# Turning raw rows by a scaled diagonal, and loading gate and up weights in row halves, in a two-layer decoder trunk

## The reference, cut to what matters

```python
def rms_norm(x, gain):
    xf = x.astype(jnp.float32)
    y = xf * lax.rsqrt(jnp.mean(xf * xf, axis=-1, keepdims=True) + NORM_EPS)
    return (y * gain.astype(jnp.float32)).astype(x.dtype)
...
    for i in range(DEPTH):
        h = rms_norm(x, attn_norm[i])
        x = x + mixer_i(h, ...)          # begins with u = h @ w_in
        h = rms_norm(x, ffn_norm[i])
        x = x + hier_moe(h, ...)
...
def expert_block(args):                  # inside hier_moe, 32 experts of width 512, top 2 per token
    xblk, e = args
    hid = jax.nn.silu(xblk @ w_gate[e]) * (xblk @ w_up[e])
    return hid @ w_down[e]
```

## Time and profile before

| | us |
|---|---|
| median of 3 runs | 1724.29 |
| lowest and highest | 1724.13, 1724.97 |
| profiled execution, its own time | 1721.84 |
| its span in the trace | 1720.0 |

### The profile page before, as it was taken

One profiled execution on the slowest core, in us unless ns is written; L12 is line 12 of the kernel. 1 busy time (PEld: TensorE's weight loads), 2 busy tenths in 40 slices (PEclk: granted clock), 3 DMA queues, 4 the chain that ended last, 5 costly groups with the idle time before them and its releaser, 6 DMA issues.

```text
span 1720.0 us, 20542 instructions
## 1 busy us (share of the span) xinstructions
PE 1584.3 (92%) x7884; PEld 749.1 (44%) x7886; DVE 440.6 (26%) x1111; ACT 393.5 (23%) x879; POOL 200.6 (12%) x287
## 2 busy tenths in 40 slices
PE   6999899799999999997499989999699999999993
PEld 3545574433333333332246457855333333333331
DVE  1485651620000000000412235643500000000002
ACT  2345450311111111111100236632211111111110
POOL 2241220000000000000101012320000000000000
PEclk9999999899999999999599999999899999999997
DMA  7120307289999999999804220043599999999995
GB/s 244 50 98 7 111 4 293 98 334 420 422 421 421 421 422 422 422 422 393 225 5 152 80 65 1 2 176 141 221 398 422 421 422 422 422 422 422 422 421 199
DMA packets 110919, 468.24 MB, mean 272 GB/s; under 512 B 34105, under 2 KB 40505, under 8 KB 61708
## 3 DMA queue, kind: packets, MB, share of 16 engines
q1 hardware_dynamic: 103564, 450.67, 65.5%
q0 software_dynamic: 5120, 8.41, 1.3%
q10 hardware_dynamic: 2176, 8.39, 1.3%
HBM read 456.91 MB, written 18.91 MB: 277 GB/s over the span
## 4 chain that ended last, share of the span: by engine, by line
PE 80%; DMA 10%; DVE 4%; SPq 2%; ACT 1%; issue 1%; POOL 1%; ACTq 0%; DVEq 0%; POOLq 0%
PE bank L1734 22%; PE bank L1747 10%; PE bank L1714 9%; PE bank L1380 8%; DMA arena<-in_moe_w_up 8%; PE bank L535 6%; PE bank L774 6%; PE bank L429 4%; PE bank L394 3%; PE bank L1724 2%; PE bank L411 2%; SPq L1686 2%; PE bank L855 2%; PE bank L1740 1%; DMA arena<-y_d 1%
## 5 line engine op out<-in xcount | busy, mean ns | idle before, releaser
L1734 PE MATMUL bank<-arena 128*64 128x512 f32 x2048 | 452.6, 594 | 17.0 <-DMA arena<-in_moe_w_up 15.5
L1734 PEld LDWEIGHTS bank<-arena 128*64 128x64 f32 x2048 | 147.6, 137 | 312.6 <-issue 303.1
L1747 PE MATMUL bank<-arena 128*64 128x512 f32 x1024 | 230.6, 592 | 2.1 <-DVE arena L1836 2.1
L1832 DVE TENSOR_TENSOR arena<-arena,bank 128x256 f32<-128x256 f32 x64 | 26.9, 421 | 656.3 <-ACT arena L1822 656.3
L1753 POOL DMA_INDIRECT y_d<-arena,slot_row x64 | 62.7, 980 | 927.8 <-ACT arena L1827 927.8
L1714 PE MATMUL bank<-arena 128*64 128x512 bf16 x1152 | 153.5, 394 | 8.2 <-DVE arena L1707 8.2
L1380 PE MATMUL bank<-arena 128*128 128x512 f32 x320 | 140.6, 601 | 0.8 <-issue 0.8
L1747 PEld LDWEIGHTS bank<-arena 128*64 128x64 f32 x1024 | 71.6, 137 | 124.4 <-issue 110.8
L1822 ACT ACTIVATE arena<-bank 128x256 f32<-128x256 f32 x64 | 24.6, 384 | 420.5 <-PE bank L1734 420.5
L535 PE MATMUL bank<-arena 128*128 128x512 f32 x256 | 111.4, 593 | 0.0
L774 PE MATMUL bank<-arena 128*128 128x512 f32 (+1 forms) x288 | 105.3, 525 | 0.0
(11 more groups left out here) (282 smaller groups left out, 1440.5 us busy)
## 6 DMA issues: line engine op xcount, KB each, us to landing
arena<-in_moe_w_gate SPq DMA_DIRECT2D x64, 2048.0 KB, 21.7
arena<-in_moe_w_up SPq DMA_DIRECT2D x64, 2048.0 KB, 26.2
arena<-in_moe_w_down SPq DMA_DIRECT2D x64, 2048.0 KB, 24.4
arena<-in_even_w_in SPq DMA_DIRECT2D x4, 2048.0 KB, 8.3
arena<-y_d ACTq DMA_DIRECT2D x8, 1024.0 KB, 8.6
arena<-bias_row_d SPq DMA_DIRECT2D x2, 3584.0 KB, 11.8
arena<-in_odd_w_in SPq DMA_DIRECT2D x3, 2048.0 KB, 7.8
arena<-in_even_w_out SPq DMA_DIRECT2D x2, 2048.0 KB, 7.8
```

The costliest lines, as they stand in the source:

```text
L1734: mm = nc.tensor.matmul(bank[1][fh * CAP:(fh + 1) * CAP, :], xeT[:, j, half * CAP:(half + 1) * CAP], wgu[u][:, :, n, fh * FH:(fh + 1) * FH ...
L1747: mm = nc.tensor.matmul(bank[3][dh * CAP:(dh + 1) * CAP, :], hidT[:, j, fh * CAP:(fh + 1) * CAP], wd[u][:, n, dh * 512:(dh + 1) * 512], st ...
```

## The change

1. Ahead of the two mixers the rows are no longer scaled before they are turned. ACT makes a 128x128 diagonal of the tile's inverse roots (`norm_diag`), and PE multiplies the raw tile by it, eight matmuls of 128x128 in the place of eight transposes. The scale 1/1024 moves into the square. Each half tile has a bank of its own, so PE doesn't wait for an eviction.
2. The norm weights lie on partitions (`acol`, two loads of 1024 single values, issued by ACT at the start), and are multiplied in at the eviction. DVE does all evictions, but for the first half of the last tile of layer 1, which ACT does in four pieces. The two broadcast loads of `attn_norm` go.
3. Ahead of `n0` each tile of x has its own semaphore, and ACT starts on the first tile as soon as it is there.
4. Of the odd layer's weight chunks only the first is loaded early; the next two are issued once the fourth load of result rows has landed. `fence` waits on the scatters' own semaphore.
5. PE runs three matmuls of 128x512, whose result nobody reads, once the first result rows are there.
6. Gate and up are loaded in row halves of 1 MB each. The first halves of expert c+3 are issued when the first 8 of the gate and up matmuls of c are done, the second halves when all are; PE waits for the second halves in the middle of its products.
7. Eight small tiles are laid into one, and the layer 1 gate logits share it.

```diff
+        acol = sb("acol", [P, 2, KD])
+        diag = split(gain[:, 0:2 * P], 2, P)
...
+            nc.scalar.activation(rows[:, i, :], xt[:, i, :], ACT.Square, scale=DM ** -0.5,
+                                 accum_out=ss[:, i:i + 1]).then_inc(S("norm_sq"), 1)
...
+        def norm_diag(act, tag, i):
+            act.wait_ge(S("norm_rstd"), NT * ORDER[tag] + i + 1)
+            if i >= 2:
+                act.wait_ge(S("turned"), 2 * NT * TURN[tag] + 2 * (i - 1))
+            nc.scalar.activation(diag[:, i % 2], ident[:], ACT.Copy, scale=rstd[:, i:i + 1]).then_inc(S("diag"), 1)
...
+        def turn_pe(pe, tag):
+            for i in range(NT):
+                pe.wait_ge(S("diag"), NT * WHOLE[tag] + i + 1)
                 for half in range(2):
-                    if i >= 2:
-                        pe.wait_ge(S(f"turn_out{half}"), NT * TURN[tag] + i - 1)
                     for k in range(4):
-                        mm = nc.tensor.transpose(bank[(2 * i + half) % 4][:, k * P:(k + 1) * P],
-                                                 src(i, 4 * half + k), ident[:])
+                        c = (4 * half + k) * P
+                        mm = nc.tensor.matmul(bank[2 * i + half][:, k * P:(k + 1) * P], xt[:, i, c:c + P], diag[:, i % 2],
+                                              start=True, stop=True)
                     mm.then_inc(S("turned"), 1)
...
+        def turn_evac(eng, tag, i, half, on_act=False):
+            eng.wait_ge(S("turned"), 2 * NT * TURN[tag] + 2 * i + half + 1)
+            d = hT[:, 4 * half:4 * half + 4, i * P:(i + 1) * P]
+            b = split(bank[2 * i + half][:, :], 4, P)
+            g = acol[:, WHOLE[tag], 4 * half:4 * half + 4]
+            if on_act:
+                for k in range(4):
+                    ins_ = nc.scalar.activation(d[:, k], b[:, k], ACT.Copy, scale=g[:, k:k + 1])
+            else:
+                ins_ = nc.vector.tensor_tensor(d, b, g.unsqueeze(2).broadcast_to((P, 4, P)), ALU.mult)
...
         def even_act(act):
-            norm_act(act, "n0", lambda e, i: e.wait_ge(S("x_in"), 16 * NT))
+            for n in range(2):
+                act.dma_start(acol[:, n, :], ins["attn_norm"][n].rearrange("(k p) -> p k", p=P)).then_inc(S("acol_in"), 16)
+            act.wait_ge(S("consts"), 1)
+            for i in range(NT):
+                act.wait_ge(S(f"x_in{i}"), 16)
+                norm_square(act, i)
+                if i >= 1:
+                    norm_diag(act, "n0", i - 1)
+            norm_diag(act, "n0", NT - 1)
...
         def odd_early(sp):
             sp.wait_ge(S("m_dn"), RING * TRIPS + 1)
-            for c in range(3):
+            load_chunk(sp, 0, OD_CHUNKS, w_odd, ow, "op", OD_JOBS)
+        def odd_next(sp):
+            sp.wait_ge(S(f"m_yin{NT - 1}"), 16)
+            for c in range(1, 3):
                 load_chunk(sp, c, OD_CHUNKS, w_odd, ow, "op", OD_JOBS)
         def odd_pe(pe):
-            turn_pe(pe, "n2", lambda i, k: rows[:, i, k * P:(k + 1) * P], lambda e, i: rows_ready(e, "n2", i + 1))
+            pe.wait_ge(S("m_yin0"), 16)
+            for _ in range(3):
+                nc.tensor.matmul(bank[7][:, :], ident[:], wd[1][:, 0, 0:512], start=True, stop=True)
+            turn_pe(pe, "n2")
...
+            for i in range(NT):
+                act.wait_ge(S("m_x"), 2 * i + 2)
+                norm_square(act, i)
+                norm_diag(act, "n2", i)
+            turn_evac(act, "n2", NT - 1, 0, True)
...
+        def one_half(sp, t, layer, e, u, n, h):
+            src = ins[("moe_w_gate", "moe_w_up")[n]][layer, bass.ds(e, 1), h * 512:(h + 1) * 512].rearrange("e (p j) f -> p e (j f)", j=4)
+            sp.dma_start(wgu[u][:, n, 4 * h:4 * h + 4].rearrange("p (e j) f -> p e (j f)", e=1), src).then_inc(S(f"{t}_{('wgu', 'wgv')[h]}{u}"), 16)
...
             pe.wait_ge(S(f"{t}_wgu{u}"), 32 * (cu + 1))
-            gate_up_mms(u).then_inc(S(f"{t}_gu"), 1)
+            gate_up_mms(u, 0).then_inc(S(f"{t}_guh"), 1)
+            pe.wait_ge(S(f"{t}_wgv{u}"), 32 * (cu + 1))
+            gate_up_mms(u, 1).then_inc(S(f"{t}_gu"), 1)
...
         def fence(eng, t, L):
-            eng.wait_ge(S(f"{t}_yfree"), NE * (L + 1) + RING)
+            eng.wait_ge(S(f"{t}_yout"), 16 * NE * (L + 1))
...
             def next_weights(c, u):
+                sp.wait_ge(S(f"{t}_guh"), c + 1 + L * NE)
+                half_weights(sp, t, L, c + RING, u, 0)
                 sp.wait_ge(S(f"{t}_gu"), c + 1 + L * NE)
-                gate_up_weights(sp, t, L, c + RING, u)
+                half_weights(sp, t, L, c + RING, u, 1)
...
             if L == 0:
-                sp.wait_ge(S(f"{t}_picked"), NE + 1)
-                sp.dma_start(gain[:], bcast_rows(ins["attn_norm"][1, :], DM)).then_inc(S("gain_in"), 16)
+                odd_next(sp)
...
-                if L == 0 and i >= 1:
-                    norm_row(dve, "n2", i - 1)
-            if L == 0:
-                norm_row(dve, "n2", NT - 1)
```

More of the change, by code:

```diff
@@ L260, in rows_ready, with norm_square @@
             eng.wait_ge(S("norm_row"), NT * NORM[tag] + tiles)
[L263 to L267, removed]
+        def norm_square(act, i):
+            nc.scalar.activation(rows[:, i, :], xt[:, i, :], ACT.Square, scale=DM ** -0.5,
+                                 accum_out=ss[:, i:i + 1]).then_inc(S("norm_sq"), 1)
         def norm_pool(pool, tag):
             for i in range(NT):
[L271 removed]
+                n = NT * ORDER[tag] + i + 1
                 pool.wait_ge(S("norm_sq"), n)
                 s_ = ss[:, i:i + 1]
[L274 removed]
+                nc.gpsimd.tensor_scalar(s_, s_, EPS, None, ALU.add).then_inc(S("norm_ms"), 1)
                 pool.wait_ge(S("norm_ms"), n)
                 nc.gpsimd.tensor_tensor(rstd[:, i:i + 1], s_, nhalf[:, 0:1], ALU.pow).then_inc(S("norm_rstd"), 1)
+        def norm_diag(act, tag, i):
[3 more added lines that the diff above has]
+            nc.scalar.activation(diag[:, i % 2], ident[:], ACT.Copy, scale=rstd[:, i:i + 1]).then_inc(S("diag"), 1)
         def norm_row(dve, tag, i):
[L280 removed]
+            dve.wait_ge(S("norm_rstd"), NT * ORDER[tag] + i + 1)
             dve.wait_ge(S("gain_in"), 16 * (NORM[tag] + 1))
@@ L764, in even_pe @@
             pe.wait_ge(S("consts"), 1)
-            turn_pe(pe, "n0", lambda i, k: rows[:, i, k * P:(k + 1) * P], lambda e, i: rows_ready(e, "n0", i + 1))
+            turn_pe(pe, "n0")
             turned(pe, "n0")
@@ L1144, in even_dve @@
             v_ = nc.vector
+            dve.wait_ge(S("acol_in"), 32)
             for i in range(NT):
-                norm_row(dve, "n0", i)
-            norm_turns(dve, "n0")
+                for half in range(2):
+                    turn_evac(dve, "n0", i, half)
             dve.wait_ge(S("ep_ev"), J_KV + 2)
@@ L1534, in odd_dve @@
             v_ = nc.vector
-            norm_turns(dve, "n2")
+            for i in range(NT):
+                for half in range(2) if i < NT - 1 else (1,):
+                    turn_evac(dve, "n2", i, half)
             for i in range(NT):
@@ L1697, in weights @@
         def weights(sp, t, layer, e, u):
-            gate_up_weights(sp, t, layer, e, u)
+            for h in range(2):
+                half_weights(sp, t, layer, e, u, h)
             down_weights(sp, t, layer, e, u)
@@ L1728, in copy_x, with gate_up_mms @@
             return nc.scalar.activation(xeT, split(bank[0][:, :], 4, P), ACT.Copy)
-        def gate_up_mms(u):
-            for n in range(KD):
+        def gate_up_mms(u, h):
+            for n in range(4 * h, 4 * h + 4):
                 half, j = n // 4, n % 4
```

56 lines of the change are left out of this document (20 added, 36 removed).

## The result

The changed kernel takes 1700.36 us (median of four runs, 1698.46 to 1701.06) against 1724.63 for the kernel before, run beside it: ratio 0.9859, 95% interval [0.9844, 0.9874]. The prediction was right: it forecast 1698 and a range of 1690 to 1709. The profiled execution took 1698.46 us with a span of 1696.6, so 23.4 us less than that of before by either number; the sum had said 26.3.

The account below looks back on a forecast made before the run. The weight stream was taken to bound the expert layers, latencies the stretch between stages. 3.4 + 7.6 + 9.9 + 5.3 + 0.1 = 26.3 us off 1721.84 gives 1695.5, with 2.45 a median of 1698; range 1690 to 1709.

Parts of the forecast that it names:

- Start of the stream: Expert layers: first halves of expert 4 issued earlier keep the weight queue whole; 1.7 us gained per layer, 3.4 for two.
- End of the stream: Expert layers' end: only 8 of 16 matmuls left after the last gate and up transfer; 7.6 us for both layers.
- Between the layers: Layer 0's last down products to layer 1's projection: scatter 3.3, fence 0.1, rows to projection 4.7, clock 1.8; 9.9 us.
- Scatter: Layer 0's scatter, 5.85 us, has only one chunk ahead in the queue, through as it starts; gain 3.3 us (0 to 3.3).
- then square 1.16: First result rows to projection: after the adds, square, POOL steps, diagonal, matmuls and eviction; 16.8 us together, gain 4.7.
- Clock: Layer 1's projection: three matmuls and the turn keep PE busy, so the clock is up before it; 1.8 us (0 to 2.6).
- The start: Kernel start: layer 0's projection starts at 19.4 instead of 24.66, after the bias table lands at 17.5; 5.3 us (2.7 to 7).
- 2.0 for the matmuls: Kernel start: matmul time counted after x's last tile, in a turn said to end at 15.2 us.
- The halves bring nothing: Expert layers: an expert's four transfers land nearly together, or the queue's gap stays; loses 3.4 + 7.1, 1708 us; chance 0.13.
- The turn and the start bring half: Start and between layers: single-value loads delay x, clock stays 0.5, diagonal lengthens the chain; 1705 us; chance 0.14.
- Smaller transfers lower the rate: Gate and up of all experts at 344 GB/s instead of 422; 130 us more, about 1828; chance 0.07.
- The estimate of 24.6 us in the place of about 13.6: Expert layers: four 1 MiB halves one after another at the skill page's 6.15 us each; the prediction set it aside.

Follow-up runs that it names:

- experiment 3: Changed kernel with both halves of gate and up issued only when all of the expert's gate and up matmuls are done; 1704.23 us, 0.9881 of before.
- experiment 5: Changed kernel with all three odd weight chunks issued early again, as before the change; 1705.69 us, 0.9891 of before.
- Experiment 7: Changed kernel with ACT squaring each tile of layer 1 before making the diagonal of the tile before; 1697.72 us, 0.9845 of before.
- experiment 6: Changed kernel without the three matmuls whose result nobody reads; 1700.09 us, 0.986 of before.
- experiment 10: Changed kernel without the three unread matmuls, layer 1's turn by transposes instead of products, inverse roots left out; 1698.95 us, one run.
- the second experiment: Kernel before with only the row halves of gate and up put in; 1716.54 us, 0.9953 of before.
- experiment 8: Changed kernel with ACT's wait for constants behind the first square and two unread matmuls ahead of the first turn; 1700.59 us, 0.9859 of before.
- experiments 8 and 11: The latter: changed kernel, squares ahead, earlier start with two unread matmuls, second `acol` load later, bias table's product behind first projection jobs; 1694.8 us, 0.9824 of before.
- experiments 1 to 3: The first of these: changed kernel with gate and up in whole 2 MB transfers, issued when all the expert's products are done; 1711.18 us, 0.9923 of before.
- experiment 9: Changed kernel with each half in two 512 KB transfers of 64 partitions, runs of 8 KB; 2395.14 us, 1.3799 of before.

## Why the prediction was right, point by point

- *Start of the stream.* 1.7 a layer predicted; experiment 3 gives 1.3 and 1.5. In layer 0 the last up half lands at 794.21 instead of 798.73, 4.52 sooner, of which 3.04 come from before the experts. The mechanism is right, the hole in the queue that closes is a little smaller than 1.7, and no other gap showed.
- *End of the stream.* 7.6 predicted: 16 records instead of 32, 3.4 in layer 0. In layer 1 the products fell from 8.73 to 3.68, 5.1 us; I had counted 4.1, with 0.6 of the 1.6 that the low clock cost, and all of it went.
- *Between the layers.* Scatter 3.3 predicted, 3.2 measured. The first result rows, which I left at 6.08, gained 0.8; experiment 5, where they take 7.99, says that the chunks' traffic reaches them too. From them to the projection 4.7 were predicted and 3.2 came (21.5 to 18.34). The step that failed is the one that began "then square 1.16": it took the last square to follow the last add. I had not looked at what stands ahead of it in ACT's queue: the diagonal of the tile before, which waits for POOL's power step. Experiment 7 shows the place and the size. Clock: 1.8 predicted, 2.5 measured (first job 9.65 to 7.14). The cause was named half wrong: the turn does it without the three matmuls, which do nothing for the total (experiment 6). That it does it by being products is shown only in part (experiment 10), and in the second experiment, with the old turn, the same 2.5 us were there by chance. The sum, 9.7 against 9.9, came out by luck: 1.5 too much on the way from the rows to the projection, 0.8 and 0.7 too little on the rows and the clock. Nor did the way itself miss by one thing: the last square started 1.9 us behind the last add, and the adds, with all rows there, took 10.5 instead of 11.1.
- *The start.* 5.3 predicted, 4.3 measured, and the mechanism was another than I had. The bound I named, the bias table at 17.5, lands where I put it (17.32 in experiment 8), but it was not the last: 64 matmuls take 9.13 us, and the product starts at 18.46. The term "2.0 for the matmuls" counted only the last tile's, as if PE kept up with x. The step that failed is this overlap; PE doesn't keep up, because its first records are slow:

```profile
8.50:10.00 1.50, 1.50 (x7) 1.50 (x8) 0.00 (x0) 1.50 (x4) 0.90 (x3) 1.00 1.08 332
10.00:12.00 2.00, 2.00 (x11) 2.00 (x11) 0.00 (x0) 0.80 (x2) 1.15 (x3) 1.00 1.10 329
12.00:14.00 2.00, 2.00 (x19) 2.00 (x18) 1.74 (x3) 0.40 (x1) 0.00 (x0) 1.00 1.21 247
```

  18 records in 3.5 us, then 19 in 2.0. It is the clock. The 1.00 of these first lines isn't a reading: the trace's first record of the clock is a rise at 12.17, and there the distance from one record to the next falls from 0.21 to 0.11 us. In experiments 8 and 11 two matmuls come first, the rise stands at 8.39 and 8.13, and the turn takes 7.4 us. Nine kernels with the same code here start the projection of layer 0 between 20.1 and 21.4, seven of them at 20.9 or later; by and large, the earlier the rise (11.55 to 14.20), the earlier the start. The profiled execution, 20.33, is one of the two early ones, so the usual miss is nearer to 2 than to 1.0. The old start moves as well: 23.30 in the second experiment, with slower first records behind it. No run separates the parts of the change at the start (own semaphores for the tiles of x, diagonal, norm weights on partitions).
- *What I left out.* The mixers lost 1.3 and 1.0 us in this pair of executions. In mixer 0 the granted clock was 0.93 between 121 and 146 us; before, it was 1.00 there. The first line is of after, the second of before:

```profile
121.00:146.00 25.00, 23.05 (x72) 12.64 (x71) 20.19 (x43) 12.49 (x24) 0.00 (x0) 0.93 0.05 11
```

```profile
121.00:146.00 25.00, 23.05 (x61) 10.44 (x60) 23.32 (x49) 11.21 (x18) 0.00 (x0) 1.00 0.03 12
```

  The change isn't the cause. From the end of the first 32 records to the first expert's products it is 303.0 us before and 304.3 after, but 302.7 to 303.0 in eight kernels with the changed code. In the third experiment it is 304.9 and in the second, which has the old code, 304.3; in these two, as in the changed kernel's profile, the clock is at 0.50 for a short time between 141 and 150. Mixer 1 takes 367.1 before and 366.9 to 369.8 in the kernels with the changed code. So 2.3 of the 2.9 us by which the sum of the table is short are scatter of single executions. Why the clock falls in some of them stays open.
- *The rivals.* "The halves bring nothing" is refuted by experiments 1 to 3. "The turn and the start bring half" holds for the start in a mild form: 4.3 of 5.3 us, or some 3.5 at the usual start. "Smaller transfers lower the rate" is false for 1 MB (422 GB/s) and begins at 512 KB with 4 KB runs (414). The 244 GB/s of experiment 9 don't bear on it: the same 512 KB are slow there by the partitions that they go to. The estimate of 24.6 us in the place of about 13.6, which stands beside it in the prediction, sets a time measured for one size against one made of a fixed part and a rate; the stream, at 422 GB/s before and after, follows neither.
- *The signs.* Of the signs of being wrong one came: a single-value load was under way when the first eviction waited for it. The second of the two `acol` loads landed at 12.2, and the first eviction started at 12.26. It cost nothing, since each half tile has a bank of its own and the last evictions follow PE.

## What to carry to other kernels

Where a stage is bound by a stream, its length is the stream plus what is left to compute after the last landing: halve the last piece's work, and find the earliest time at which its first transfer can be issued, but measure the rate when pieces get smaller. When a wait is taken away between stages, write down for each engine what stands ahead of the last instruction in its queue: here a square behind a diagonal cost 1.6 us, and a bias table that became last turned a faster start into one at the low clock. Matmuls that only raise the clock are worth trying where PE is idle ahead of slow work: at the kernel's start two of them took 1.7 us off the turn, between the layers three of them gave nothing, since the turn raised the clock in time by itself. And before a difference of a microsecond between two traces is explained, look at how far apart other traces of the same code lie.

## What the runs showed of the hardware

- 64-partition transfers move 244 GB/s where 128-partition ones move 422, even with the two sets alternately in one queue (experiment 9); both show a full share (1.02 and 1.01), so the share doesn't reveal it.
- The first matmul records of the program take 0.21 us each and later ones 0.11; the step falls on the trace's first record of the clock (12.17 us here, 11.55 to 14.20 in others). The stretches list 1.00 ahead of it, where the trace has no record.
- Transposes raised the granted clock in the second experiment, at 16.89 us (from 0.21 to 0.11 us for each) and at 846.33, just ahead of the projection.
- POOL's power step on 128 single values takes 1.5 us while DVE adds, and 0.57 when it doesn't (in order of time, in the changed kernel):

```profile
817.28 1.49 POOL L279 TENSOR_TENSOR rstd<-ss,nhalf 128x1 f32<-128x1 f32 x1
...
824.59 0.57 POOL L279 TENSOR_TENSOR rstd<-ss,nhalf 128x1 f32<-128x1 f32 x1
```

- The two loads of 1024 single values issued beside x landed so late that the first eviction waited for them until 12.26 us in the changed kernel and 12.44 in experiment 8; where only one was issued ahead, the first eviction began at 9.83, with the turn starting at 8.56 (8.31 in experiment 8).
